# First feed-forward: six plain tile pairs, then sixteen pairs by seven block products

## The chip, the cores and the metric

One core of one Trainium2 chip runs the whole program in one launch. The metric is the device time in microseconds (us), the median of several runs. The engines are PE (matmul), DVE, ACT and POOL (elementwise), and SP, which issues the loads from HBM; PEld is PE's weight load.

## The reference, cut to what matters

The program is three transformer-like blocks over 512 tokens of width 1024. The change touches the feed-forward of the first:

```python
D_FF = 2816
def swiglu(h, w1, w2):
    g, u = jnp.split(h @ w1, 2, axis=-1)
    return (jax.nn.silu(g) * u) @ w2
...
h_lat = h_lat + g2 * swiglu(modulate(rms_norm(h_lat, norm2_g[l]), sh2, sc2),
                            w_ffn_in[l], w_ffn_out[l])
```

Beside it the kernel computes modulation rows for later use, `silu(c) @ w_ada + b_ada` (the sixth group of the first block's and the three groups `w_ada_3` of the third block's), as running sums of 128x1024 rows.

## The kernel before

**Numbers.** Everything is held transposed, features on the 128 partitions and 512 tokens along a row. A float32 operand is held as two parts, high (rounded to fp32r) and low (the rest). A product is three matmuls: high x high, high x low and low x high (L1477 to L1479 for 512 columns). A weight tile of 128x1024 is loaded to one of five buffers (`raw`, t_53; `NRAW` = 5, L206), cast by ACT (L1914) and subtracted by POOL (L3179), which gives its high and low part. The event `read` of a load is the end of its last reader. `send` (L1333) issues load number n only after `read` of load n - 5; SP does this in order. ACT casts the tile two ahead in its own order (`LOOK`).

**The feed-forward.** There are 22 pairs: gate tile g(i) and up tile u(i), 8 input tiles each. `ffn` (L687) takes them in two parts, each followed by the output products (e and d) over the middle tiles of that part. There are two forms:
- `plain` (L757), in the first block's feed-forward (tag ff1) alone, in parts of 14 and 8 pairs: 48 matmuls of 512 columns a pair. Behind the products come silu on ACT (L2218), gate times up on DVE (L2949), the high part on ACT (L2006), the low part on DVE (L2422).
- `fours` (L802), in the four feed-forwards of the second block, in parts of 8 and 14 pairs. Gate, up and the two halves of the tokens form a 2x2 block product that is done by seven block products p1, p5, p6, p7, p4, p2, p3 in this order: 84 matmuls of 256 columns (L1513 to L1515). The seven weight pieces of a pair (A11, S1, S2, S3, A22, A12, S4) are 128x512: S1 to S4 are sums made by DVE from both raw tiles of the pair (U the upper, L the lower), L2432, L2435, L2445; pieces are cast by ACT (L1929) and their low parts made by POOL (L3189) or DVE (L2452). The results are put together on DVE: `second_sum`, `third_sum`, `up_sum` (L2472; p3 waits for it), `last_sum` (L2477), L2484 (a scaling that ff1 doesn't have), `pair_up` (L2494), `mid_low` (L2422). The pieces of pair i+1 are made during pair i. In DVE's queue S1 of pair i+1 stands ahead of `second_sum` and `up_sum` of pair i.

**Order.** It is written out by hand in the loops. Each engine is in order. The generator `modulations` (L545) makes one step each time `next(m.side)` is called: eight steps with one load of w_ada (R) and one sum on DVE (L2543 for the first, L2546), an empty one, and one that closes the group (16 small matmuls on PE, L1782, and one DVE add). The sums' `read` frees their raw buffer. In ff1 it is called once in each pair from the fourth on, and two to four times beside each output tile.

**Weight parts.** Three buffers for high and low parts are taken in turn in ff1, four in the other feed-forwards (`rotate`); a block piece takes half of one.

## Time and profile before

| | us |
|---|---|
| median of three runs | 3389.88 (3387.67 to 3390.45) |
| the profiled execution, its own time | 3392.9 |
| its span | 3391.1 |
| first matmul of ff1 to the first of the next block | 835.46 to 1208.42 |

Starts in the rows are in us from the span's start. A line number is the line that issued an instruction. In square brackets stands the idle time of the engine before a row, and what ended it.

### The profile page before, as it was taken

The numbers are of one execution on the slowest core, as the hardware profiler recorded it, in microseconds if no ns is written. First come the engines' busy times: TensorE is split into PE (matmuls) and PEld (weight loads), VectorE is DVE, ScalarE is ACT, GpSimd is POOL, SyncE is SP. The second block draws the span as 40 slices with busy tenths as digits, with TensorE's granted clock in tenths as the row PEclk, the third lists the DMA queues.
The fourth block names the chain that finished last, engine by engine and source line by source line (L and its number), as shares of the span: only waits on it lengthen the run. The fifth ranks groups of instructions, "written<-read, shape, count | busy, mean of one in ns | idle before, by whom it ended". The sixth has DMA issues, their size and how long they took to land.

```text
span 3391.1 us, 47136 instructions
## 1 busy us (share of the span) xinstructions
PE 3309.1 (98%) x18750; PEld 2794.0 (82%) x18750; DVE 1872.6 (55%) x3335; ACT 1416.2 (42%) x2517; POOL 1680.6 (50%) x996
## 2 busy tenths in 40 slices
PE   8999999999999999999999999999999989999998
PEld 5767788887888898988777999899987769998776
DVE  4266775433222386842667576557624667682655
ACT  4533323423322353533445354444434455352643
POOL 4323445554544455655525565565646346564432
PEclk9999999999999999999999999999999999999999
DMA  7212334442344423234312323332343113233221
GB/s 285 69 51 63 95 98 131 148 143 75 123 154 137 151 94 100 100 104 116 85 35 89 102 100 105 95 112 88 107 109 111 32 60 116 96 109 99 73 63 56
DMA packets 102218, 345.95 MB, mean 102 GB/s; under 512 B 12174, under 2 KB 12558, under 8 KB 101839
## 3 DMA queue, kind: packets, MB, share of 16 engines
q1 hardware_dynamic: 101200, 341.10, 31.4%
q8 instruction: 148, 2.42, 0.3%
q10 hardware_dynamic: 798, 1.85, 0.2%
q14 instruction: 72, 0.58, 0.1%
HBM read 336.08 MB, written 2.10 MB: 100 GB/s over the span
## 4 chain that ended last, share of the span: by engine, by line
PE 88%; DVE 5%; ACT 3%; POOL 1%; DMA 1%; issue 1%; SPq 0%; DVEq 0%; ACTq 0%
PE ps L1477 17%; PE ps L1479 16%; PE ps L1478 16%; PE ps L1513 8%; PE ps L1514 8%; PE ps L1515 8%; PE ps L1540 2%; PE ps L1541 2%; PE ps L1542 2%; PE ps L1827 2%; PE ps L1854 1%; PE ps L1837 1%; ACT t L1929 1%; PE ps L1746 1%; POOL t L3179 1%
## 5 line engine op out<-in xcount | busy, mean ns | idle before, releaser
L3179 POOL TENSOR_TENSOR t<-t,t 128x1024 fp32r<-128x1024 f32 (+2 forms) x408 | 923.2, 2269 | 1162.2 <-ACT t L1914 1153.0
L1477 PE MATMUL ps<-t,t 128*128 128x512 f32 x2608 | 1046.2, 401 | 11.6 <-POOL t L3179 5.9
L1479 PE MATMUL ps<-t,t 128*128 128x512 f32 x2608 | 1026.1, 393 | 0.0
L1478 PE MATMUL ps<-t,t 128*128 128x512 f32 x2608 | 1025.1, 393 | 0.0
L3189 POOL TENSOR_TENSOR t<-t,t 128x512 fp32r<-128x512 f32 x440 | 572.2, 1329 | 361.7 <-ACT t L1929 361.7
L1513 PE MATMUL ps<-t,t 128*128 128x256 f32 x2464 | 695.7, 282 | 18.4 <-POOL t L3189 7.1
L1514 PE MATMUL ps<-t,t 128*128 128x256 f32 x2464 | 694.9, 282 | 0.0
L1515 PE MATMUL ps<-t,t 128*128 128x256 f32 x2464 | 693.7, 282 | 0.0
L1477 PEld LDWEIGHTS ps<-t,t 128*128 128x128 f32 x2608 | 493.1, 189 | 140.7 <-issue 23.9
L1479 PEld LDWEIGHTS ps<-t,t 128*128 128x128 f32 x2608 | 492.3, 189 | 110.3
L1478 PEld LDWEIGHTS ps<-t,t 128*128 128x128 f32 x2608 | 493.1, 189 | 103.8 <-issue 1.7
L1914 ACT CAST t<-t 128x1024 fp32r<-128x1024 f32 (+2 forms) x412 | 398.9, 977 | 359.8 <-PE ps L1479 223.0
L1513 PEld LDWEIGHTS ps<-t,t 128*128 128x128 f32 x2464 | 466.4, 189 | 24.3 <-POOL t L3189 10.2
L1515 PEld LDWEIGHTS ps<-t,t 128*128 128x128 f32 x2464 | 466.6, 189 | 0.0
L1514 PEld LDWEIGHTS ps<-t,t 128*128 128x128 f32 x2464 | 465.1, 189 | 0.3
L1929 ACT CAST t<-t 128x512 fp32r<-128x512 f32 x440 | 255.5, 620 | 201.6 <-DVE t L2445 180.9
L2259 ACT ACTIVATE t<-ps,t 128x128 f32<-128x128 f32 (+3 forms) x160 | 86.6, 545 | 199.4 <-DVE t L3021 86.7
L1929 ACT CAST t<-ps 128x512 fp32r<-128x512 f32 x176 | 103.5, 588 | 145.0 <-DVE ps L2435 106.6
L2722 DVE SCALAR_TENSOR_TENSOR ps<-t,t,ps 128x392 f32<-128x392 f32 (+14 forms) x232 | 159.1, 686 | 6.2
L2445 DVE TENSOR_TENSOR t<-t,ps 128x512 f32<-128x512 f32 x176 | 120.2, 683 | 48.4 <-PE ps L1515 44.0
L1540 PE MATMUL ps<-t,t 128*128 128x512 f32 x336 | 134.9, 401 | 5.4 <-DVE t L2630 2.8
L2452 DVE TENSOR_TENSOR t<-ps,t 128x512 fp32r<-128x512 f32 x176 | 120.9, 687 | 30.8 <-ACT t L1929 27.8
(325 smaller groups left out, 3613.3 us busy)
## 6 DMA issues: line engine op xcount, KB each, us to landing
t<-in_w_f1i SPq DMA_DIRECT2D x88, 512.0 KB, 3.8
t<-in_w_f2i SPq DMA_DIRECT2D x88, 512.0 KB, 3.7
t<-in_w_ada SPq DMA_DIRECT2D x72, 512.0 KB, 4.3
t<-in_w_ffi SPq DMA_DIRECT2D x44, 512.0 KB, 3.7
t<-in_w_f1o SPq DMA_DIRECT2D x32, 512.0 KB, 4.0
t<-in_w_f2o SPq DMA_DIRECT2D x32, 512.0 KB, 4.1
t<-in_w_gate SPq DMA_DIRECT2D x24, 512.0 KB, 4.2
t<-in_w_out SPq DMA_DIRECT2D x48, 256.0 KB, 2.6
```

The lines of the kernel that those rows point to most:

```text
L1477: e.matmul(out, wh[:, at], X.hi[c][:, 0:N], start=c == first, stop=False)
L1478: e.matmul(out, wh[:, at], X.lo[c][:, 0:N], start=False, stop=False)
L1479: m = e.matmul(out, wl[:, at], X.hi[c][:, 0:N], start=False, stop=c == final)
L1513: e.matmul(out, wh[:, at], m.A.hi(j, x), start=opens and j == 0, stop=False, skip_group_check=not opens)
L1514: e.matmul(out, wh[:, at], m.A.lo(j, x), start=False, stop=False, skip_group_check=not opens)
L1515: mm = e.matmul(out, wl[:, at], m.A.hi(j, x), start=False, stop=j == 3, skip_group_check=not opens)
L1540: e.matmul(out, X.hi[c][:, at], wh[:, w], start=c == 0, stop=False)
L1914: e.copy(k.WH[k.slot[n]][:, 0:w], k.raw[:, j % NRAW, 0:w]).then_inc(*k.rounded.inc(('rounded', j)))
L1929: e.copy(four(piece_at(k, k.WH, m, i, piece)), src).then_inc(*k.rounded.inc(('rounded', m.tag, i, piece)))
L2722: e.scalar_tensor_tensor((c3 if j == 30 else a3)[:, :, lo:hi], h3[:, :, lo + w - 15:hi + w - 15], param(k, 'conv_w', w * 8 + i), a3[:, :, ...
L3179: e.tensor_tensor(k.WL[k.slot[n]][:, 0:w], k.raw[:, j % NRAW, 0:w], f(k.WH[k.slot[n]][:, 0:w]), ALU.subtract).then_inc(*k.rest.inc(('rest' ...
L3189: e.tensor_tensor(four(piece_at(k, k.WL, m, i, piece)), src, four(f(piece_at(k, k.WH, m, i, piece))), ALU.subtract).then_inc(*k.rest.inc(( ...
```

## The change

ff1 is now six plain pairs (0 to 5) and then block pairs: 6 and 7 in part 0, 8 to 21 in part 1, so that the output tiles take 8 middle tiles in part 0 and 14 in part 1 (before 14 and 8).

The block form needs sums of input blocks (t1 to t4, `Turned`). They are made beside pairs 1 to 4 by `turn_even` and `turn_odd`: per step four copies on ACT (512, 256, 512 and 256 columns) and ten sums on DVE (four of 512 and six of 256 columns), ordered around `ffn_gate` and `ffn_up`. The first four pieces of pair 6 are begun beside pair 5 (`begin_pair`).

`next(m.side)` is called twice in each of the six plain pairs, twice beside each output tile of part 0, once in each of the pairs 8 to 13, and as before in part 1's output tiles. Silu of a block pair reads PSUM directly. The ring of temporary tiles for the middle is three instead of four.

```diff
@@ -204,7 +229,7 @@
 
 
 NRAW, LOOK, LEAD = (5, 2, 2)
-PARTS, PAIRS = (((0, 14), (14, 8)), ((0, 8), (8, 14)))
+PAIRS, PLAIN = (((0, 8), (8, 14)), 6)
 PIECES = ('A11', 'S1', 'S2', 'S3', 'A22', 'A12', 'S4')
 PRODUCTS = {'p1': ('A11', 'b11', 'A', 0), 'p5': ('S1', 't1', 'D', 256), 'p6': ('S2', 't2', 'B', 0), 'p7': ('S3', 't3', 'C', 0), 'p4': ('A22', 't4', 'D', 0), 'p2': ('A12', 'b21', 'A', 0), 'p3': ('S4', 'b22', 'D', 256)}
 SUMS = ('b11', 't1', 't2', 't3', 't4', 'b21', 'b22')
@@ -318,6 +343,13 @@
     k.MH, k.ML = k.MH + k.MH[0:8], k.ML + k.ML[0:8]
     high = sbuf(k, [128, 4, 7 * 256], F32R, at=k.halves)
     first, outer, low = sbuf(k, [128, 1024], F32R, at=k.halves + 28 * 1024), place(k, 0, [128, 768], F32R), place(k, 3, [128, 3, 7 * 256], F32R)
+    turned, last = place(k, -6, [128, 30, 256], F32R), place(k, 88, [128, 2, 256], F32R)
+    sets = []
+    for j in range(7):
+        p = 4 * j
+        sets.append([turned[:, p, :], turned[:, p + 1, :], turned[:, p + 2, :], turned[:, p + 3, :], turned[:, p + 1:p + 3, :].rearrange('p a n -> p (a n)')])
+    sets.append([last[:, 0, :], turned[:, 28, :], turned[:, 29, :], last[:, 1, :], turned[:, 28:30, :].rearrange('p a n -> p (a n)')])
+    k.TH, k.TL = (sets[0:4], sets[4:8])
     k.SUMH = [high[:, j, :] for j in range(4)]
     k.SUML = [(first, outer)] + [(low[:, j, 0:1024], low[:, j, 1024:1792]) for j in range(3)]
 
@@ -633,16 +665,16 @@
     m = Norm(res.sum, k.X, lambda j: ('x', 'out1', j), A, lambda j: k.sm[:, j:j + 1], lambda j: k.ada[:, 24 + j:25 + j], [('filled', ('out1', 7)), ('gain2',)], keep=True, bank=True)
     for j in range(11):
         norm(on, m, j)
-    twin = short(banked(Sum('f1_0', k.R[0], S, ('normed', 'n2', 7), range(8), 0, [('lo', ('mid', 'ff1'), FF - 1)])))
-    first = banked(Sum('fin1', k.R[1], S, ('normed', 'cn', 7), range(8)))
+    twin = short(banked(Sum('f1_0', k.R[0], S, ('filled', ('u', 'ff1', FF - 1)), range(8), 0, [('lo', ('mid', 'ff1'), FF - 1)])))
+    first = banked(Sum('fin1', k.R[1], S, ('filled', ('u', 'ff1', FF - 1)), range(8)))
     first.slots = twin.slots
     on.final_gain()
     on.twin_gain('final_g', 2)
     res = Residual('ff1', lambda j: k.ada[:, 40 + j:41 + j], first, [('ada', 'ada', 5)], None, Sums(k, 'f1_0'), lambda j: k.sm[:, 16 + j:17 + j], twin, lambda j: k.sm[:, 24 + j:25 + j])
-    m = Ffn('ff1', 'ffi', 'ffo', A, None, res, [('filled', ('out1', 7))], side=side)
+    m = Ffn('ff1', 'ffi', 'ffo', A, None, res, [('filled', ('out1', 7))], side=side, clear=('filled', ('out1', 7)))
+    m.sums, m.start = (Turned(k, A), PLAIN)
     m.next = Ffn('f1_0', 'f1i0', 'f1o0', res.A, twin, None, [('filled', ('d', 'ff1', 7))], res, clear=('filled', ('out1', 7)), before=res)
     ffn(on, k, m)
-    on.rotate(8, 0)
     return m.next
@@ -660,13 +692,14 @@
     def __init__(self, tag, wi, wo, A, scale, res, since, whole=None, side=iter(()), clear=None, before=None):
         self.tag, self.wi, self.wo, self.A, self.scale, self.res, self.since, self.whole = (tag, wi, wo, A, scale, res, since, whole)
         self.side, self.next, self.clear, self.before = (side, None, clear, before)
+        self.sums, self.start = (A, 0)
 
     def again(self, i):
 
         return [('filled', ('e', self.tag, KT - 1))] if i >= 14 else []
 
...
@@ -686,9 +719,12 @@
 
 def ffn(on, k, m):
     m.mid = Pair(('mid', m.tag), k.MH, k.ML)
-    for part, (first, count) in enumerate(PARTS if m.scale is None else PAIRS):
-        (plain if m.scale is None else fours)(on, m, first, count)
-        after = (m.next, 0) if part else (None if m.scale is None else m, first + count)
+    for part, (first, count) in enumerate(PAIRS):
+        if first < m.start:
+            plain(on, m)
+            on.rotate(8, 0)
+        fours(on, m, max(first, m.start), first + count - max(first, m.start))
+        after = (m.next, 0) if part else (m, first + count)
         for n in range(KT):
             on.T(('ed'[part], m.tag, n), m.wo, n, m.mid, kt=count, first=first)
             for _ in range(n < 4 if part else 2):
@@ -754,17 +790,25 @@
         on.add_squares(res, n)
 
 
-def plain(on, m, first, count):
-    for i in range(first, first + count):
+def plain(on, m):
+    for i in range(m.start):
         if i:
             on.T(('g', m.tag, i), m.wi, i, m.A)
         else:
             on.T2((('g', m.tag, 0), m.wi, 0), (('u', m.tag, 0), m.wi, FF), m.A)
         on.ffn_gate(m, i)
+        if 0 < i < 5:
+            on.turn_even(m, i - 1)
+        if i == m.start - 1:
+            begin_pair(on, m, m.start, KT - 2)
         if i:
             on.T(('u', m.tag, i), m.wi, FF + i, m.A)
         on.ffn_up(m, i)
-        if i > 2:
+        if 0 < i < 5:
+            on.turn_odd(m, i - 1)
+        if i == m.start - 1:
+            begin_pair(on, m, m.start, KT - 1)
+        for _ in range(2):
             next(m.side, None)
 
 
@@ -860,6 +904,8 @@
             on.round(m, i + 1, 'S4')
             on.minus(m, i + 1, 'S4')
         on.product(m, i, 'p3')
+        if 7 < i < 14:
+            next(m.side, None)
         if m.whole is not None and i == 2:
             on.roots(m.whole.sum, 1)
         if m.whole is not None and i == 3:
...
@@ -1509,10 +1559,10 @@
             self.wait_ge('up sum', m.tag, i)
         for j in js:
             at = slice(128 * j, 128 * j + 128)
-            self.wait_ge('lo', m.A.tag, j, x)
-            e.matmul(out, wh[:, at], m.A.hi(j, x), start=opens and j == 0, stop=False, skip_group_check=not opens)
-            e.matmul(out, wh[:, at], m.A.lo(j, x), start=False, stop=False, skip_group_check=not opens)
-            mm = e.matmul(out, wl[:, at], m.A.hi(j, x), start=False, stop=j == 3, skip_group_check=not opens)
+            self.wait_ge(*m.sums.ready(j, x))
+            e.matmul(out, wh[:, at], m.sums.hi(j, x), start=opens and j == 0, stop=False, skip_group_check=not opens)
+            e.matmul(out, wh[:, at], m.sums.lo(j, x), start=False, stop=False, skip_group_check=not opens)
+            mm = e.matmul(out, wl[:, at], m.sums.hi(j, x), start=False, stop=j == 3, skip_group_check=not opens)
         if js[-1] == 3:
             mm.then_inc(*k.filled.inc(('used', m.tag, i, piece), ('filled', (p, m.tag, i)), *([('filled', ('u', m.tag, i))] if p == 'p3' else [])))
 
@@ -1916,7 +1974,7 @@
     def round(self, m, i, piece):
 
         k, e = (self.k, self.e)
-        if i == 0:
+        if i == m.start:
             self.wait_ge(*m.clear)
         for event in k.before.get((m.tag, i, piece), ()):
             self.wait_ge(*event)
@@ -1931,14 +1989,22 @@
     def first_copy(self, m, i):
         k, e = (self.k, self.e)
         self.wait_ge('filled', ('p1', m.tag, i))
-        if i:
+        if i > m.start:
             self.wait_ge('last sum', m.tag, i - 1)
+        elif m.start:
+            self.wait_ge('normed', m.A.tag, 7)
         else:
             self.wait_ge('x', m.before.tag, 7)
         e.copy(k.tmp[3][:, 0:256], self.bank('A', m.tag, i)[:, 0:256]).then_inc(*k.act.inc(('first copy', m.tag, i)))
 
     def pair_gate(self, m, i):
-        self.ffn_gate(m, i)
+        k, e = (self.k, self.e)
+        if m.scale is not None:
+            self.ffn_gate(m, i)
+            return
+        b = self.take(m.ring(k), 'm', m.tag, i)
+        self.wait_ge('last sum', m.tag, i)
+        e.activation(b, self.bank('A', m.tag, i), ACT.Silu).then_inc(*k.act.inc(('silu', m.tag, i), ('free', ('A', m.tag, i))))
 
     def pair_up(self, m, i):
         self.high(m.mid, i, self.bank('C', m.tag, i), ('up', m.tag, i), *m.since, *m.again(i))
@@ -2177,6 +2243,22 @@
         else:
             e.activation(A.hi(j, 'b21', 2), x, ACT.Copy, scale=g).then_inc(*k.act.inc(('hi', A.tag, j, 'b2')))
 
+    def turn_even(self, m, j):
+        k, e, A, T, b = (self.k, self.e, m.A, m.sums, self.bank('G', m.tag, j))
+        self.lent('G', m.tag, j)
+        self.wait_ge('lo', A.tag, 2 * j + 1)
+        e.copy(pairs(b), f(k.HH)[:, 2 * j:2 * j + 2, 256:512]).then_inc(*k.act.inc(('turn high', j)))
+        for event in (m.clear, ('filled', ('row', A.tag))):
+            self.wait_ge(*event)
+        self.wait_ge('turned', j, 't1')
+        e.copy(T.hi(j, 't1'), b[:, 0:256]).then_inc(*k.act.inc(('hi', A.tag, j, 't1')))
+
+    def turn_odd(self, m, j):
+        k, e, A, T, b, c = (self.k, self.e, m.A, m.sums, self.bank('G', m.tag, j), self.bank('H', m.tag, j))
+        self.wait_ge('turned', j, 't4')
+        e.copy(T.hi(j, 't2', 2), b).then_inc(*k.act.inc(('hi', A.tag, j, 't2')))
+        e.copy(T.hi(j, 't4'), c[:, 0:256]).then_inc(*k.act.inc(('hi', A.tag, j, 't4')))
+
     def sum_highs(self, res, n):
 
         k, e, A, j, b = (self.k, self.e, res.A, n // 2, self.bank('G', res.A.tag, n // 2))
@@ -2478,6 +2560,8 @@
 
     def pair_gate(self, m, i):
         k, e = (self.k, self.e)
+        if m.scale is None:
+            return
         b = self.take(m.ring(k), 'm', m.tag, i)
         self.wait_ge('row', m.scale.tag)
         self.wait_ge('last sum', m.tag, i)
@@ -2835,6 +2919,36 @@
         if j % 2:
             self.low(A, j, self.k.O[:, j, :])
 
+    def turn_even(self, m, j):
+
+        k, e, A, T, b = (self.k, self.e, m.A, m.sums, self.bank('G', m.tag, j))
+        self.wait_ge('turn high', j)
+        e.tensor_tensor(b, b, f(A.hi[2 * j]), ALU.subtract).then_inc(*k.dve.inc())
+        self.settle()
+        e.tensor_tensor(pairs(b), pairs(b), f(k.HL)[:, 2 * j:2 * j + 2, 256:512], ALU.add).then_inc(*k.dve.inc())
+        self.settle()
+        e.tensor_tensor(b, b, f(A.lo[2 * j]), ALU.subtract).then_inc(*k.dve.inc(('turned', j, 't1')))
+
+    def turn_odd(self, m, j):
+
+        k, e, A, T, b, c = (self.k, self.e, m.A, m.sums, self.bank('G', m.tag, j), self.bank('H', m.tag, j))
+        one, three, hi, lo = (b[:, 0:256], c[:, 0:256], f(A.hi[2 * j + 1]), f(A.lo[2 * j + 1]))
+        self.wait_ge('hi', A.tag, j, 't1')
+        e.tensor_tensor(T.lo(j, 't1'), one, f(T.hi(j, 't1')), ALU.subtract).then_inc(*k.dve.inc(('lo', A.tag, j, 't1')))
+        self.settle()
+        e.tensor_tensor(one, hi[:, 256:512], one, ALU.subtract).then_inc(*k.dve.inc())
+        self.settle()
+        e.tensor_tensor(one, lo[:, 256:512], one, ALU.add).then_inc(*k.dve.inc())
+        self.settle()
+        self.lent('H', m.tag, j)
+        e.tensor_tensor(three, hi[:, 0:256], one, ALU.subtract).then_inc(*k.dve.inc())
+        self.settle()
+        e.tensor_tensor(three, lo[:, 0:256], three, ALU.add).then_inc(*k.dve.inc(('turned', j, 't4')))
+        self.wait_ge('hi', A.tag, j, 't2')
+        e.tensor_tensor(T.lo(j, 't2', 2), b, f(T.hi(j, 't2', 2)), ALU.subtract).then_inc(*k.dve.inc(('lo', A.tag, j, 't2'), ('lo', A.tag, j, 't3'), ('free', ('G', m.tag, j))))
+        self.wait_ge('hi', A.tag, j, 't4')
+        e.tensor_tensor(T.lo(j, 't4'), three, f(T.hi(j, 't4')), ALU.subtract).then_inc(*k.dve.inc(('lo', A.tag, j, 't4'), ('free', ('H', m.tag, j))))
+
     def sum_parts(self, res, n):
 
         k, e, A, g, j, x, b = (self.k, self.e, res.A, res.g(n), n // 2, self.k.X[:, n, :], self.bank('G', res.A.tag, n // 2))
```

SP's queue at the start of ff1. Tile t_53 is the five raw buffers, in_w_ffi the gate and up weights, in_w_ada the modulation rows. Before:

```order
L1341 DMA t_53<-in_w_out 128x1024 x8
L1341 DMA t_53<-in_w_ffi 128x1024 x8
L1341 DMA t_53<-in_w_ada 128x1024
L1341 DMA t_53<-in_w_ffi 128x1024 x2
L1341 DMA t_53<-in_w_ada 128x1024
L1341 DMA t_53<-in_w_ffi 128x1024 x2
```

With the change:

```order
L1391 DMA t_53<-in_w_out 128x1024 x8
L1391 DMA t_53<-in_w_ffi 128x1024 x2
L1391 DMA t_53<-in_w_ada 128x1024 x2
L1391 DMA t_53<-in_w_ffi 128x1024 x2
L1391 DMA t_53<-in_w_ada 128x1024 x2
L1391 DMA t_53<-in_w_ffi 128x1024 x2
L1391 DMA t_53<-in_w_ada 128x1024 x2
L1391 DMA t_53<-in_w_ffi 128x1024 x4
```

Two ada loads now follow each pair's two weight loads; before, eight weight loads came first and one ada load per pair after them.

DVE's queue from the product of pair 1 to that of pair 2 (t_63 and t_64 are middle tiles, t_126 the turned sums, t_50 and t_51 the input's high and low parts, t_56 the running sum). Before:

```order
L2949 TENSOR_TENSOR t_63<-t_63,ps 128x512 [waits s_act,s_filled]
L2422 TENSOR_TENSOR t_121<-t_63,t_120 128x512 [waits s_act]
L2949 TENSOR_TENSOR t_64<-t_64,ps 128x512 [waits s_act,s_filled]
L2422 TENSOR_TENSOR t_121<-t_64,t_120 128x512 [waits s_act]
```

With the change:

```order
L3063 TENSOR_TENSOR t_63<-t_63,ps 128x512 [waits s_filled]
L2504 TENSOR_TENSOR t_121<-t_63,t_120 128x512 [waits s_act]
L2937 TENSOR_TENSOR t_126<-ps,t_126 128x256
L2939 TENSOR_TENSOR ps<-t_50,ps 128x256 [waits s_dve]
L2941 TENSOR_TENSOR ps<-t_51,ps 128x256 [waits s_dve]
L2944 TENSOR_TENSOR ps<-t_50,ps 128x256 [waits s_dve]
L2946 TENSOR_TENSOR ps<-t_51,ps 128x256 [waits s_dve]
L2948 TENSOR_TENSOR t_126<-ps,t_126 128x512 [waits s_act]
L2950 TENSOR_TENSOR t_126<-ps,t_126 128x256 [waits s_act]
L2630 SCALAR_TENSOR_TENSOR t_56<-t_53,t_60,t_56 128x1024 [waits s_raw4]
L2630 SCALAR_TENSOR_TENSOR t_56<-t_53,t_60,t_56 128x1024 [waits s_dve,s_raw0]
L2926 TENSOR_TENSOR ps<-ps,t_50 128x512 [waits s_act]
```

The two sums of ada loads (s_raw4, s_raw0) stand behind the pair's product, its low part and the turned sums.

DVE's queue around the end of the block pair 8, with the change (t_65 holds the partial results, t_64 a middle tile):

```order
L2554 TENSOR_TENSOR ps<-ps,t_65 128x512 [waits s_dve,s_filled]
L2527 TENSOR_TENSOR t_55<-t_53,ps 128x512 [waits s_dve,s_filled]
L2627 TENSOR_SCALAR t_56<-t_53,t_60 128x1024 [waits s_raw1]
L2559 TENSOR_TENSOR ps<-ps,t_65 128x256 [waits s_filled]
L2514 TENSOR_TENSOR ps<-t_53 128x512 [waits s_raw1,s_raw0,s_act]
L2578 TENSOR_TENSOR ps<-t_64,ps 128x512 [waits s_dve]
```

These are up_sum, S4 of the next pair, the ada sum, last_sum, S1 of the pair after, pair_up. The ada sum and S1 use the same raw buffer (s_raw1). Before, ff1 had no block pairs, and no block pair elsewhere has an ada sum.

## Rows read from the trace of the kernel before

**Rows 1.** The page: span, busy time of PE, the chain's share by engine.
```profile
span 3391.1 us, 47136 instructions
...
PE 3309.1 (98%) x18750; PEld 2794.0 (82%) x18750; DVE 1872.6 (55%) x3335; ACT 1416.2 (42%) x2517; POOL 1680.6 (50%) x996
...
PE 88%; DVE 5%; ACT 3%; POOL 1%; DMA 1%; issue 1%; SPq 0%; DVEq 0%; ACTq 0%
```

**Rows 2.** Timeline of DVE, plain pairs: start, duration, line, tiles, idle before.
```profile
852.24 0.69 DVE L2422 TENSOR_TENSOR t<-t,t 128x512 fp32r<-128x512 f32 x1 [0.69 <-ACT t L2006]
860.03 0.69 DVE L2949 TENSOR_TENSOR t<-t,ps 128x512 f32<-128x512 f32 x1 [7.10 <-PE ps L1479]
861.41 0.69 DVE L2422 TENSOR_TENSOR t<-t,t 128x512 fp32r<-128x512 f32 x1 [0.69 <-ACT t L2006]
870.91 0.69 DVE L2949 TENSOR_TENSOR t<-t,ps 128x512 f32<-128x512 f32 x1 [8.81 <-PE ps L1479]
...
881.79 0.69 DVE L2949 TENSOR_TENSOR t<-t,ps 128x512 f32<-128x512 f32 x1 [8.81 <-PE ps L1479]
...
883.77 1.28 DVE L2546 SCALAR_TENSOR_TENSOR t<-t,t,t 128x1024 f32<-128x1024 f32 x1
```

**Rows 3.** Timeline of DVE, block pairs of the second block.
```profile
1399.80 0.43 DVE L2477 TENSOR_TENSOR ps<-ps,t 128x256 f32<-128x256 f32 x1 [0.73 <-PE ps L1515]
...
1400.88 1.81 DVE L2432 TENSOR_TENSOR ps<-t 128x512 f32<-128x512 f32 x1
...
1407.13 0.69 DVE L2472 TENSOR_TENSOR ps<-ps,t 128x512 f32<-128x512 f32 x1
1408.31 0.69 DVE L2445 TENSOR_TENSOR t<-t,ps 128x512 f32<-128x512 f32 x1 [0.49 <-PE ps L1515]
1409.73 0.43 DVE L2477 TENSOR_TENSOR ps<-ps,t 128x256 f32<-128x256 f32 x1 [0.72 <-PE ps L1515]
...
1419.65 0.43 DVE L2477 TENSOR_TENSOR ps<-ps,t 128x256 f32<-128x256 f32 x1 [0.75 <-PE ps L1515]
```

**Rows 4.** SP's timeline, and time to landing of ffi's 44 loads.
```profile
885.08 0.33 SPq L1341 DMA_DIRECT2D t<-in_w_ffi  x1
...
DMA to landing us min/median/max: 3.4/3.7/5.8
```

**Rows 5.** Timeline of ACT in plain pairs, and one copy in a block pair.
```profile
852.12 1.05 ACT L1914 CAST t<-t 128x1024 fp32r<-128x1024 f32 x1
854.59 0.60 ACT L2218 ACTIVATE t<-ps 128x512 f32<-128x512 f32 x1 [1.43 <-PE ps L1479]
...
1401.53 0.36 ACT L1938 COPY t<-ps 128x256 f32<-128x256 f32 x1
```

**Rows 6.** Timeline of POOL, splits of weight tiles in plain pairs.
```profile
853.24 2.39 POOL L3179 TENSOR_TENSOR t<-t,t 128x1024 fp32r<-128x1024 f32 x1 [1.90 <-ACT t L1914]
...
884.16 3.15 POOL L3179 TENSOR_TENSOR t<-t,t 128x1024 fp32r<-128x1024 f32 x1 [3.81 <-ACT t L1914]
```

**Rows 7.** Timeline of PE, one of the four closings of a modulation group.
```profile
957.76 1.84 PE L1782 MATMUL ps<-t 128*128 128x2 f32 x16
```

**Rows 8.** Timeline of DVE beside an output tile of ff1, two ada sums.
```profile
1044.65 4.62 DVE L2546 SCALAR_TENSOR_TENSOR t<-t,t,t 128x1024 f32<-128x1024 f32 x2
```

**Rows 9.** Groups of DVE by line, 1345 to 1475 us: busy, mean ns, idle.
```profile
L2432 DVE TENSOR_TENSOR ps<-t 128x512 f32<-128x512 f32 x12 | 17.1, 1425 | 0.0
L2435 DVE TENSOR_TENSOR ps<-ps,t 128x512 f32<-128x512 f32 x13 | 9.1, 700 | 0.4
```

**Rows 10.** PE's timeline at ff1's start; busy by engine, granted clock, DMA there.
```profile
835.46 0.77 PE L1477 MATMUL ps<-t,t 128*128 128x512 f32 x1 [2.45 <-DVE t L2592]
...
829.00:840.00 11.00, 6.62 (x21) 5.44 (x21) 7.05 (x12) 4.99 (x8) 0.00 (x0) 0.53 0.01 2
```

**Rows 11.** The same view by stretches, the next blocks' first pairs.
```profile
1208.00:1224.00 16.00, 13.37 (x105) 12.48 (x104) 14.30 (x25) 9.50 (x19) 9.77 (x7) 1.00 0.19 66
2172.00:2188.00 16.00, 13.36 (x105) 12.48 (x104) 13.98 (x22) 7.42 (x15) 8.55 (x6) 1.00 0.23 67
```

30 lines of the change are left out of this document (27 added, 3 removed).

## The prediction

> **What bounds the kernel now.** I read the page's head first [rows 1]: TensorE (PE) is busy 98% of the span and holds 88% of the chain that ended last; DVE, ACT and POOL are near half. A change pays only through the length of PE's queue or through PE's waits. So I went to the first block's feed-forward, 835 to 1208 us, and asked two things: how long a pair (one gate and one up tile) takes PE in either form, and how near the other engines are to making PE wait.
>
> Pace. In the plain tiles the gate-times-up product on DVE (L2949) stands at 860.03, 870.91, 881.79 [rows 2]: 10.88 us a pair, 48 products of 512 columns, with PE busy for all of it. In block form the last sum (L2477) stands at 1399.80, 1409.73, 1419.65 [rows 3]: 9.93 us for 84 products of 256 columns. I use those distances and not counts of matmul records, since some records are missing. A pair saves 0.95 us, not an eighth of 10.88 (1.36), because a short product pays its fixed part more often.
>
> Waits. Weights pass through five load buffers. A load may be issued only when the load five before it has been read. The trace shows this wait: DVE reads an ada load from 883.77 for 1.28 us [rows 2], and SP issues the next ffi load at 885.08 [rows 4], 0.03 us later. A load lands 3.7 us after issue (median) [rows 4]; then ACT's cast (1.05) and POOL's subtraction (2.4) must end before PE may use it: 3.51 us from 852.12 to 855.63 [rows 5, 6]. So a load is usable 7.2 us after its buffer is read. Before, with one ada load per pair, and only from pair 3, the load five later has over a pair of room and PE never waits for it.
>
> **The change, part by part.**
>
> Sixteen pairs in block form: 16 x 0.95 = 15.2 us off PE's queue (14 to 16 by the spread of the distances). The output tiles keep 176 x 3 products. Four closings of 1.84 us on PE [rows 7] stay four.
>
> Two ada loads in each of pairs 0, 1, 2, 4 and 5. The loads now run g, u, R, R (R an ada load; L and U for a block pair are below), four a pair, so g of pair i+2 takes the buffer of the second R of pair i. That R is read by DVE behind all DVE work of pair i, which begins when pair i is complete on PE. Its g must be usable one pair (10.88) later. Room for DVE: 10.88 - 7.2 = 3.7 us. What stands there: the product, the wait for ACT's high part and the low part, 2.1 us (860.03 to 862.10) [rows 2], and two ada sums of 1.28: 4.6 already. With turn_odd: six sums of 256 columns at about 0.43, one of 512 at 0.69, a 0.6 us ACT copy between [rows 2, 3, 5]: 4 us more.
> - Pair 2: R0b follows the low part that ends at 852.93, so it is read at 855.5, g2 usable at 862.8; pair 1 ends at 860.0 (its product on DVE is at 860.03). Wait 2.9 us (2.5 to 3.5).
> - Pair 3: ACT stands in order at the cast of g2 till 859.2, before silu of pair 1 and the first turn copy. Then follow cast 1.05, silu 0.6, copy 0.6, turn_even's three sums (2.1), copy 0.4, the cast of u2, product and high and low, turn_odd 4, two ada sums: R1b is read near 872.5, g3 usable at 879.8, against 862.8 + 10.88 = 873.7. Wait 6.1 us (4.5 to 8).
> - Pair 3 issues no R (its steps are an empty one and a closing), so g4 takes u2's buffer and u4 R2a's: both are usable 0.5 to 2 us early, and pair 5 likewise.
> - Pair 6, the first block pair: U6 takes R4b's buffer. DVE after pair 4: 2.1 + 4 + 2.6, so U6 lands 12.4 us after pair 4's end; A11 needs ACT 0.6 and POOL 1.3 more: 14.4 against 10.88, wait 3.5. S2 comes behind pair 5's product on DVE: 1.5. L7 takes R5a's buffer, read after that: S1 of pair 7 stands in DVE's queue until L7 lands, and up_sum of pair 6, for which p3 waits, is behind it: 4.6. Together 9.6 (3.2 to 12). The low end has no late load: A11's first half buffer is last used by u5, so cast and subtraction (2.0) are exposed anyway, with 1.2 for S2.
>
> Output tiles of part 0: now 5.44 us each with three loads, before 9.7 with four. Two ada sums took 4.62 us there against 2 x 1.28 alone [rows 2, 8]. With the 0.75 us residual step that is 5.4 of 5.44 us. I take 1.5 us (0 to 6).
>
> Pairs 8 to 13: one R each, between L of i and U of i+1. L of i+2 takes R of i's buffer. DVE's order in a pair: last_sum(i-1), S1(i+1), product(i-1), and so on to up_sum(i), S4(i+1), the ada sum. Measured from a pair's start on PE (1399.7): up_sum ends at 8.1 and p3 may begin at 8.5; S4 runs 8.6 to 9.3 [rows 3]. So the ada sum ends at 10.6 or later, 0.6 into the next pair; L lands at 4.4; S1 starts then instead of at 1.2; from its end to up_sum's end was 5.13 us (1402.69 to 1407.82) back to back [rows 3]: 10.2 + 0.1 against 8.5: p3 waits 1.8 us, and the next pair repeats it. S1, with both inputs in SBUF, takes 1.42 us on the mean against 0.68 to 0.70 for sums from PSUM [rows 9]; an ada sum has the same inputs, so I take 2.0 a pair (0 to 2.4). Only L10 to L14 are hit (o7 is in front of L9's slot, L13 in front of L15's): 5 x 2.0 = 10.0.
>
> The Trainium skill, "SBUF — State Buffer", section "SBUF: two separate sides", says that a DVE operation with two SBUF inputs and a GpSimd operation exclude each other for a whole instruction. The trace agrees: POOL's split under an ada sum took 3.15 against 2.40 [rows 6]. By that rule alone every ada sum could wait out a split of 2.4, which would put the case at the dear rival's time below.
>
> Clock. Where PE last waited in pieces, 2.45 us before 835.46 among them, the granted clock was 0.53 over 829 to 840, the 1.2 GHz level for nearly all of it [rows 10]: up to 5 us for one such stretch. The new gaps are as long or longer. Where a late load sets the next start anyway the slower PE is hidden; after pair 3's start it isn't. I take 3 us (0 to 10). The skill's "TensorE: Matmul & The Clock Gate", section "HAM oscillation — how this bites in real kernels", has the same rule against waiting PE; by it the first three waits would each bring a slow stretch, 5 us more than my sum.
>
> The next block's first pair: 1208 to 1224 and 2172 to 2188 have the same PE busy time (13.37, 13.36) [rows 11], the first behind eight-part, the second behind fourteen-part output tiles. So the longer tiles of part 1 buy nothing there: 0 (-1 to +1). The rings of three instead of four, the priors of the two square sums and the rotation are free: what they wait for is long done.
>
> Sum: 2.9 + 6.1 + 9.6 + 1.5 + 10.0 + 3.0 = 33.1 of waits, less 15.2: **+17.9 us**. The profiled execution took 3392.9 us with a span of 3391.1; the median of the three runs is 3389.9, and against it this gives **3407.8**.
>
> **The rivals.**
> - *No buffer is late* (faster). It needs DVE to read the second ada load within 3.7 us of a pair's end. Then only pair 6's 3.2 us stay: 3389.9 - 15.2 + 3.2 = 3378. For it: DVE had stood idle 8.81 us before the product at 870.91 [rows 2]. Against it: that idle time lies before PE ends the pair, and the work behind that point is 8.7 us long. 0.11.
> - *The inner waits are absorbed.* The plain tiles and pair 6 behave as forecast, but S1's delay in pairs 9 to 13 hides in DVE's idle 1.4 us a pair and less work without a scaled gate: 10 less, 3398, down to 3393 if pair 6 is cheap too. 0.17.
> - *Collisions and clock come dear*: each ada pair 4.6 us (+2 at pairs 2, 3, 6), output tiles +4, clock +5: 3423. 0.16.
> - *Nothing moves* (the extra waits come to just the saving): 3390. It needs waits of half my sum. 0.06.
>
> **How the numbers follow.** Forecast 0.50: 3400 to 3416 by its own bounds. The likeliest is 3407.8. Leaving out the fast rival and part of the dear one, 3391 to 3424 holds 8 in 10. A measurement can tell some 0.2% (6.8 us) from no change. Faster: 0.11. Within: 0.06 and a third of the absorbed case, 0.12. Slower: the rest, 0.77.
>
> **What the profile after would show.** L2949's successors no longer 10.88 apart: gaps before pairs 2 and 3 of 3 and 6 us, with ACT waiting for a DMA of ffi and POOL for ACT. In the block pairs 9 to 13, 11.9 us between last sums, PE's p3 waiting for up_sum, S1 idle before it for a DMA; pairs 14 to 21 at 9.93. PE's queue is 576 matmuls longer. If pairs 2 and 3 start on time, the reading of the five buffers is wrong and the fast rival holds.

## The result, and the profile after

The changed kernel takes **3433.98 us** (median of four runs, 3430.47 to 3435.73) against 3390.16 of the kernel before, run beside it: a ratio of 1.0122, 95% interval 1.011 to 1.0135. The forecast was 3407.8 with a range of 3391 to 3424: the sign was right, the size was not, and the time lies 10 us above the range. The profiled executions differ by 39.4 us (spans of 3430.5 and 3391.1).

The page of the changed kernel, the rows that answer to [rows 1]:

```profile
span 3430.5 us, 48764 instructions
...
PE 3308.1 (96%) x19326; PEld 2817.3 (82%) x19326; DVE 2000.0 (58%) x3535; ACT 1457.7 (42%) x2629; POOL 1703.0 (50%) x1044
...
PE 84%; DVE 8%; ACT 4%; DMA 2%; issue 1%; POOL 1%; SPq 0%; DVEq 0%; ACTq 0%
```

PE is as busy as before (3308 against 3309 us) with 576 matmuls more, and holds 84% of the chain instead of 88%. DVE, ACT and DMA have taken its place: PE waits more. Where, the stretches show (us, busy time of each engine with its count, granted clock, DMA share). They are the plain pairs, pairs 6 and 7, the output tiles of part 0, pairs 8 to 21, the output tiles of part 1:

```profile
833.86:928.58 94.72, 74.82 (x304) 59.86 (x305) 55.00 (x75) 28.44 (x45) 27.72 (x13) 0.90 0.30 100
928.58:958.82 30.24, 24.37 (x168) 23.58 (x169) 17.61 (x25) 11.77 (x20) 18.35 (x11) 0.88 0.38 122
958.82:1008.76 49.94, 48.71 (x226) 39.39 (x225) 26.21 (x26) 9.29 (x11) 16.03 (x7) 1.00 0.59 200
1008.76:1162.55 153.79, 143.12 (x1178) 142.07 (x1178) 113.20 (x170) 75.51 (x137) 98.07 (x71) 0.99 0.37 119
1162.55:1242.83 80.28, 79.74 (x354) 65.01 (x353) 31.99 (x58) 33.60 (x55) 32.75 (x16) 1.00 0.34 101
```

ff1 takes 408.97 us from its first product to the next block's, before 372.96: 36.0 of the 39.4 us. Before, the same six plain pairs took 68.0 us (835.46 to 903.47); now 94.7, one closing among it.

PE's timeline, the rows with a wait before pairs 2 and 3, before and in pair 6, and in pair 10:

```profile
862.45 0.80 PE L1527 MATMUL ps<-t,t 128*128 128x512 f32 x1 [4.06 <-POOL t L3293]
...
883.19 0.77 PE L1527 MATMUL ps<-t,t 128*128 128x512 f32 x1 [7.16 <-POOL t L3293]
...
928.58 0.56 PE L1563 MATMUL ps<-t,t 128*128 128x256 f32 x1 [7.79 <-POOL t L3303]
934.28 0.39 PE L1563 MATMUL ps<-t,t 128*128 128x256 f32 x1 [0.89 <-DVE t L2534]
936.61 0.39 PE L1563 MATMUL ps<-t,t 128*128 128x256 f32 x1 [0.63 <-POOL t L3303]
938.83 0.39 PE L1563 MATMUL ps<-t,t 128*128 128x256 f32 x1 [0.55 <-POOL t L3303]
945.74 0.36 PE L1563 MATMUL ps<-t,t 128*128 128x256 f32 x1 [3.79 <-DVE ps L2554]
...
1042.90 0.35 PE L1563 MATMUL ps<-t,t 128*128 128x256 f32 x1 [2.84 <-DVE ps L2554]
```

The places are those of the forecast. The waits before pairs 2, 3 and 6 are longer than forecast (4.06, 7.16 and 7.79 us against 2.9, 6.1 and 3.5); the four inside pair 6 come to 5.9 against 6.1. What stands behind the one before pair 3, on DVE, SP, ACT and POOL (L3063 is gate times up, [rows 2]; L2504 the low part; L2630 two ada sums):

```profile
863.07 0.68 DVE L3063 TENSOR_TENSOR t<-t,ps 128x512 f32<-128x512 f32 x1
865.06 2.44 DVE L2504 TENSOR_TENSOR t<-t,t 128x512 fp32r<-128x512 f32 x1 [1.32 <-ACT t L2072]
871.29 2.66 DVE L2630 SCALAR_TENSOR_TENSOR t<-t,t,t 128x1024 f32<-128x1024 f32 x2
...
873.98 19.59 SPq L1391 DMA_DIRECT2D t<-in_w_ffi  x4
...
879.58 1.04 ACT L1972 CAST t<-t 128x1024 fp32r<-128x1024 f32 x1 [8.99 <-DMA t<-in_w_ffi]
...
864.59 2.37 POOL L3293 TENSOR_TENSOR t<-t,t 128x1024 fp32r<-128x1024 f32 x1 [2.19 <-ACT t L1972]
880.70 2.35 POOL L3293 TENSOR_TENSOR t<-t,t 128x1024 fp32r<-128x1024 f32 x1 [13.74 <-ACT t L1972]
```

DVE's second ada sum ends at 873.95, SP issues g3 at 873.98, ACT can cast it only 5.6 us later, and POOL's split ends at 883.05: the chain of the forecast, link by link. Two links were longer. The low part took 2.44 us and not 0.69: POOL's split ends at 866.96, and DVE's low part ends 0.54 later. And the load came after 5.6 us, not 3.7 [rows 4]; of the twelve ffi loads from 835 to 960 the median to landing is 6.0.

One sentence of the section on the kernel has to be put right: a step of the modulations is not made "two to four times beside each output tile" but twice beside each tile of part 0 and once beside each of the first four of part 1. The forecast's sum doesn't use it.

### The profile page after: what moved, and what is told of

It reads as the page before. It is cut to its first block, busy times and chain, and to the rows that moved or that the text cites. A ratio compares the mean times of both kernels' runs of the same rounds, so it can differ in the third digit from the quotient of the medians.

```text
span 3430.5 us, 48764 instructions
## 1 busy us (share of the span) xinstructions
PE 3308.1 (96%) x19326; PEld 2817.3 (82%) x19326; DVE 2000.0 (58%) x3535; ACT 1457.7 (42%) x2629; POOL 1703.0 (50%) x1044
## 4 chain that ended last, share of the span: by engine, by line
PE 84%; DVE 8%; ACT 4%; DMA 2%; issue 1%; POOL 1%; SPq 0%; DVEq 0%; ACTq 0%
PE ps L1527 14%; PE ps L1529 14%; PE ps L1528 14%; PE ps L1563 9%; PE ps L1564 9%; PE ps L1565 9%; PE ps L1590 2%; PE ps L1592 2%; PE ps L1591 2%; PE ps L1885 2%; PE ps L1912 1%; DMA t<-in_w_ffi 1%; ACT t L1987 1%; PE ps L1895 1%; DVE t L2630 1%
## 5 line engine op out<-in xcount | busy, mean ns | idle before, releaser
L3293 POOL TENSOR_TENSOR t<-t,t 128x1024 fp32r<-128x1024 f32 (+1 forms) x376 | 837.4, 2235 | 1088.4 <-ACT t L1972 1078.9
L1527 PE MATMUL ps<-t,t 128*128 128x512 f32 x2352 | 949.4, 404 | 24.8 <-POOL t L3293 18.9
L1529 PE MATMUL ps<-t,t 128*128 128x512 f32 x2352 | 927.8, 394 | 0.0
L1528 PE MATMUL ps<-t,t 128*128 128x512 f32 x2352 | 927.2, 394 | 0.0
L3303 POOL TENSOR_TENSOR t<-t,t 128x512 fp32r<-128x512 f32 x520 | 680.3, 1336 | 452.1 <-ACT t L1987 452.1
L1563 PE MATMUL ps<-t,t 128*128 128x256 f32 x2912 | 825.8, 284 | 44.0 <-DVE ps L2554 20.1
L1564 PE MATMUL ps<-t,t 128*128 128x256 f32 x2912 | 823.9, 283 | 0.0
L1565 PE MATMUL ps<-t,t 128*128 128x256 f32 x2912 | 822.7, 283 | 0.0
L1563 PEld LDWEIGHTS ps<-t,t 128*128 128x128 f32 x2912 | 554.6, 190 | 52.4 <-issue 30.3
L1527 PEld LDWEIGHTS ps<-t,t 128*128 128x128 f32 x2352 | 446.2, 190 | 146.4 <-issue 33.9
L1565 PEld LDWEIGHTS ps<-t,t 128*128 128x128 f32 x2912 | 554.3, 190 | 0.0
L1564 PEld LDWEIGHTS ps<-t,t 128*128 128x128 f32 x2912 | 552.9, 190 | 0.3
L1529 PEld LDWEIGHTS ps<-t,t 128*128 128x128 f32 x2352 | 445.4, 189 | 100.3
L1528 PEld LDWEIGHTS ps<-t,t 128*128 128x128 f32 x2352 | 446.4, 190 | 93.5 <-issue 1.7
L1972 ACT CAST t<-t 128x1024 fp32r<-128x1024 f32 (+2 forms) x380 | 364.7, 971 | 334.3 <-PE ps L1529 180.5
L1987 ACT CAST t<-t 128x512 fp32r<-128x512 f32 x520 | 302.4, 620 | 249.5 <-DVE t L2527 217.4
L2527 DVE TENSOR_TENSOR t<-t,ps 128x512 f32<-128x512 f32 x208 | 141.8, 682 | 54.3 <-PE ps L1565 49.3
L2534 DVE TENSOR_TENSOR t<-ps,t 128x512 fp32r<-128x512 f32 x208 | 142.7, 686 | 35.6 <-ACT t L1987 31.8
L2514 DVE TENSOR_TENSOR ps<-t 128x512 f32<-128x512 f32 x104 | 139.5, 1341 | 27.4 <-DMA t<-in_w_ffi 27.2
```

Source lines behind the costliest of these rows:

```text
L1527: e.matmul(out, wh[:, at], X.hi[c][:, 0:N], start=c == first, stop=False)
L1528: e.matmul(out, wh[:, at], X.lo[c][:, 0:N], start=False, stop=False)
L1529: m = e.matmul(out, wl[:, at], X.hi[c][:, 0:N], start=False, stop=c == final)
L1563: e.matmul(out, wh[:, at], m.sums.hi(j, x), start=opens and j == 0, stop=False, skip_group_check=not opens)
L1564: e.matmul(out, wh[:, at], m.sums.lo(j, x), start=False, stop=False, skip_group_check=not opens)
L1565: mm = e.matmul(out, wl[:, at], m.sums.hi(j, x), start=False, stop=j == 3, skip_group_check=not opens)
```

## The experiments

Theory 1 is the forecast's: late modulation reads keep load buffers from weight tiles. Theory 2: the turned sums and the block form's own work make PE wait, whatever the loads. Theory 3: DVE or DMA can't carry that many loads a pair, in any order. All ratios below are against the kernel before, which took 3392.86 to 3393.00 us beside these runs, with the 95% interval.

Behind ff1 all these kernels have the same code. Yet from ff1's end to the end of the program the profiled executions took 2182.7 us in the kernel before, 2187.7 in the changed one, and 2182.7 to 2188.2 in the runs below. So some us of each median come from outside ff1, and an edit is better read by ff1's own length (408.97 us in the changed kernel), which stands with each run.

**Both kernels without most modulation loads.** The edit, the same in both:

```diff
                 for kt in range(KT):
-                    on.ada_sum(name, g, kt)
+                    (kt in (0, 7) or (name, g) in (('ada', 2), ('ada', 3), ('ada', 4))) and on.ada_sum(name, g, kt)
                     yield
...
-            self.wait_ge('ada part', name, g, kt - 1)
+            self.wait_ge('ada part', name, g, kt - 1 if (name, g) in (('ada', 2), ('ada', 3), ('ada', 4)) else 0)
```

> The changed kernel with work left out: of the modulation group that is summed in ff1 and of the three groups of the third block only the first and the last row (kt 0 and 7) are loaded and summed, so 24 loads and 24 DVE sums are gone and the order of all else stays. Theory 1 (late loads: a modulation load that DVE reads late holds the buffer of a weight load): nothing is late in pairs 2, 3 and 9 to 13, block form is worth its 15.2 us less 3 to 5 at pair 6, and this kernel takes 3375 to 3382 us, some 55 less than with all loads (3434). Theory 2 (the turned sums and the block form's own DVE and POOL work make PE wait, whatever the loads): pairs 2 and 3 still wait 3 us or more each and the time stays above 3400.

> The kernel before with the same 24 loads and sums left out. Both theories: its pairs are 10.88 us apart with or without them, so 3387 to 3390 us, the base against which the other cut kernel is read. The distance between the two cut kernels is what block form itself brings: 10 to 12 us by theory 1, none or less than none by theory 2.

The changed kernel so cut took 3385.83 us (0.9979, 0.997 to 0.9989), the one before 3391.51 (0.9993, 0.9984 to 1.0003), both above what was expected (3375 to 3382, and 3387 to 3390). The stretches of the changed one:

```profile
835.20:907.21 72.01, 69.46 (x304) 57.05 (x305) 42.73 (x71) 29.26 (x46) 27.94 (x13) 0.97 0.26 88
907.21:929.75 22.54, 21.79 (x169) 21.62 (x169) 12.77 (x21) 11.08 (x19) 16.48 (x11) 0.92 0.38 121
929.75:977.63 47.88, 47.88 (x227) 39.64 (x225) 15.08 (x17) 9.06 (x11) 16.58 (x7) 1.00 0.31 109
977.63:1118.51 140.88, 140.49 (x1178) 140.32 (x1178) 107.27 (x165) 76.04 (x137) 93.50 (x71) 1.00 0.34 112
```

The loads, their sums and what they trigger are the loss: 48 us by the medians (3434.0 to 3385.8), 45.4 of them in ff1 (408.97 to 363.59). The waits before pairs 2 and 3 are gone, the turned sums still made. That speaks against theory 2. But block form itself brings only 5.7 us between the two cut kernels, not the 10 to 12 expected. In ff1 it is 8.5 (372.10 against 363.59), which adds up: 16 x 0.87 = 13.9, since the last sums of L2559 stand 10.01 apart here and not 9.93 [rows 3]; less 2.1 for the wait for the first block piece (907.21, the low end of the forecast for pair 6), 2.5 in pairs 6 and 7, 0.8 in pairs 8 to 21. The other 2.8 us are lost outside ff1, as shown below.

The cut changed kernel also shows DVE and POOL meeting, with no load in the way (low parts L2504; splits L3293):

```profile
861.15 0.85 DVE L2504 TENSOR_TENSOR t<-t,t 128x512 fp32r<-128x512 f32 x1 [0.69 <-ACT t L2072]
872.03 1.56 DVE L2504 TENSOR_TENSOR t<-t,t 128x512 fp32r<-128x512 f32 x1 [0.69 <-ACT t L2072]
882.92 2.25 DVE L2504 TENSOR_TENSOR t<-t,t 128x512 fp32r<-128x512 f32 x1 [0.69 <-ACT t L2072]
...
859.05 2.40 POOL L3293 TENSOR_TENSOR t<-t,t 128x1024 fp32r<-128x1024 f32 x1 [3.65 <-ACT t L1972]
870.64 2.40 POOL L3293 TENSOR_TENSOR t<-t,t 128x1024 fp32r<-128x1024 f32 x1 [2.13 <-ACT t L1972]
882.24 2.38 POOL L3293 TENSOR_TENSOR t<-t,t 128x1024 fp32r<-128x1024 f32 x1 [1.33 <-ACT t L1972]
```

The splits end at 861.45, 873.04 and 884.62, the low parts at 862.00, 873.59 and 885.17: always 0.55 us later, whenever the low part began. It doesn't run slower; it stands still until POOL is done. The rule of the Trainium skill that the forecast weighed ("SBUF — State Buffer", "SBUF: two separate sides") says this: a DVE operation with two SBUF inputs and a GpSimd one lock each other out for a whole instruction. The trace agrees.

Such a meeting is also behind the 2.8 us outside ff1. In the next block an operation of DVE (L3158) has two SBUF inputs and takes 0.75 us in the other cut kernel. Here a split begins 0.04 us after it:

```profile
1637.96 2.93 DVE L3158 SCALAR_TENSOR_TENSOR t<-t,t,t 128x512 f32<-128x512 f32 x1
1638.00 2.34 POOL L3293 TENSOR_TENSOR t<-t,t 128x1024 fp32r<-128x1024 f32 x1 [0.43 <-ACT t L1972]
1641.63 0.88 PE L1895 MATMUL ps<-t,t 128*128 128x128 f32 x3 [3.17 <-DVE t L3100]
```

It ends at 1640.89, again 0.55 us after the split. PE waits 3.17 us for the DVE operation behind it, in the other kernel 0.98, and the granted clock of the next 8 us is 0.81, there 1.00: by the end of these products the lead has fallen from 7.7 us to 4.0 in the profiled executions. Whether the two met in every execution isn't recorded.

**Loads one place earlier.**

```diff
             on.T2((('g', m.tag, 0), m.wi, 0), (('u', m.tag, 0), m.wi, FF), m.A)
+        for _ in range(2):
+            next(m.side, None)
         on.ffn_gate(m, i)
...
             begin_pair(on, m, m.start, KT - 1)
-        for _ in range(2):
-            next(m.side, None)
```

> All work is done. In the six plain pairs the two modulation steps stand between the gate and the up tile, no longer behind the up tile; as many loads, one place earlier, and the DVE sums behind the turned sums as before. Theory 1: the buffer that was kept from a gate tile is now kept from an up tile, which is needed 5.44 us later, so a lateness of 4 and 7 us at pairs 2 and 3 becomes 0 to 2, and at pair 6 only 3 to 4 us of the 10 stay: 15 to 24 us less than the changed kernel, 3410 to 3419. Theory 3 (DVE or the DMA queue can't do two loads a pair in any order): less than 5 us of change.

3408.95 us (1.0047, 1.0032 to 1.0062), 25 less than the changed kernel with the same loads and the same work, and 1 below the expected range; ff1 took 389.66 us, 19.3 less. Theory 3 is out for the plain pairs. The stretches of plain pairs and of pairs 6 and 7:

```profile
833.60:915.72 82.12, 72.28 (x304) 58.02 (x305) 61.98 (x79) 29.07 (x46) 30.70 (x13) 0.95 0.36 119
915.72:938.26 22.54, 21.86 (x169) 21.69 (x170) 12.77 (x21) 11.08 (x19) 16.55 (x11) 0.92 0.45 153
```

12.6 us come back in the plain pairs and 7.7 in pairs 6 and 7, which are as short as with the loads left out.

**No loads in pairs 8 to 13.**

```diff
-            for _ in range(n < 4 if part else 2):
+            for _ in range((2, 2, 2, 2, 1, 1, 0, 0)[n] if part else 2):
...
-        if 7 < i < 14:
+        if False:
             next(m.side, None)
```

> The changed kernel with no modulation step in pairs 8 to 13; instead ten steps instead of four beside the output tiles of part 1 (2, 2, 2, 2, 1, 1, 0, 0). All work is done. Pairs 9 to 13 took 12.4 to 13.1 us between last sums where pairs 14 to 21 took 10.0. If the one modulation load a pair is the cause, they come to 10.0: 5 x 2.8 = 14 us less, less one or two half-clock stretches on the way, 2 to 4 us more in the tiles of part 1: 3420 (3416 to 3424). If it is the block form itself (S1 from two SBUF inputs, the read of the turned sums), they stay above 12 and the time at 3431 to 3436.

3420.29 us (1.0082, 1.0068 to 1.0095), 13.7 less, as theory 1 said. Pairs 8 to 21 take 140.88 us instead of 153.79, to 0.01 us what they take with the loads left out; the output tiles of part 1 take 2.6 more, the plain pairs, which the edit leaves as they are, 1.4. ff1 took 400.07 us, 8.9 less.

**The same loads, read one place earlier in DVE's queue in pairs 8 to 13.**

```diff
         on.up_sum(m, i)
+        if 7 < i < 14:
+            next(m.side, None)
         on.product(m, i, 'p2')
...
         on.product(m, i, 'p3')
-        if 7 < i < 14:
-            next(m.side, None)
```

> The changed kernel with the modulation step of pairs 8 to 13 one place earlier in DVE's queue: behind up_sum, ahead of S4 of the next pair, so that DVE reads the load 1.2 us earlier, ahead of S4's wait for p4; the same loads in the same order. If p3 waits because the load behind it in the ring is issued late (SP waits for that read), each of the five pairs gets 1 to 1.3 us shorter (12.8 to 11.6), 5 to 7 us in all, 3427 to 3429. If DVE is simply full in these pairs (its sums take 2.35 us there and not 1.28), nothing changes, within 2 us of 3434.

3425.87 us (1.0099, 1.0086 to 1.0113), 8 less and 1 below the expected range. But ff1 took 406.11 us, only 2.9 less, pairs 8 to 21 in it 3.3 less (150.46 against 153.79): most of the 8 us lies outside ff1, and that the median came near the range is luck. Last sums of L2559 stood 12.78, 13.09, 12.77, 12.41 and 12.88 apart (63.9 us); now 12.06, 13.50, 10.32, 11.91 and 12.18 (60.0). Up to the last sum of pair 14 the gain is 3.3 us. So 3 to 4 us came back here, less than the 5 to 7 expected; a slow stretch lies in these pairs in both kernels (granted clock 0.57 from 1055 to 1059 before the edit, 0.63 from 1043 to 1047 with it). The changed kernel first, then this one:

```profile
1030.16 2.35 DVE L2630 SCALAR_TENSOR_TENSOR t<-t,t,t 128x1024 f32<-128x1024 f32 x1
1032.43 0.42 DVE L2559 TENSOR_TENSOR ps<-ps,t 128x256 f32<-128x256 f32 x1
1036.92 0.70 DVE L2514 TENSOR_TENSOR ps<-t 128x512 f32<-128x512 f32 x1 [4.07 <-DMA t<-in_w_ffi]
...
1042.06 0.69 DVE L2554 TENSOR_TENSOR ps<-ps,t 128x512 f32<-128x512 f32 x1
1042.66 0.68 DVE L2527 TENSOR_TENSOR t<-t,ps 128x512 f32<-128x512 f32 x1
1043.26 2.35 DVE L2630 SCALAR_TENSOR_TENSOR t<-t,t,t 128x1024 f32<-128x1024 f32 x1
```

```profile
1029.74 1.70 DVE L2630 SCALAR_TENSOR_TENSOR t<-t,t,t 128x1024 f32<-128x1024 f32 x1
1031.36 0.67 DVE L2527 TENSOR_TENSOR t<-t,ps 128x512 f32<-128x512 f32 x1
```

The first fence is a closed loop: ada sum 2.35, load 4.4 to S1, 6.4 from S1 to the end of S4, next ada sum. That is 13.1 us from one ada sum to the next, and PE has no part in it but to wait for up_sum. With the ada sum at 1.28 the loop would be 12.0, which is the forecast's 11.9. Moving the read ahead of S4 shortens the loop by S4's 0.6 and by what the sum no longer waits for POOL (1.70, mean 1.65 in these pairs, against 2.35).

**Turned sums shortened.** In `turn_even` and `turn_odd` on DVE:

```diff
-        e.tensor_tensor(pairs(b), pairs(b), f(k.HL)[:, 2 * j:2 * j + 2, 256:512], ALU.add).then_inc(*k.dve.inc())
-        self.settle()
...
-        e.tensor_tensor(one, hi[:, 256:512], one, ALU.subtract).then_inc(*k.dve.inc())
-        self.settle()
-        e.tensor_tensor(one, lo[:, 256:512], one, ALU.add).then_inc(*k.dve.inc())
-        self.settle()
...
-        e.tensor_tensor(three, hi[:, 0:256], one, ALU.subtract).then_inc(*k.dve.inc())
-        self.settle()
-        e.tensor_tensor(three, lo[:, 0:256], three, ALU.add).then_inc(*k.dve.inc(('turned', j, 't4')))
+        e.tensor_tensor(three, hi[:, 0:256], one, ALU.subtract).then_inc(*k.dve.inc(('turned', j, 't4')))
```

> The changed kernel with part of the computation left out: of the seven DVE sums a step between product and product that make the turned blocks the ones that bring in the low part and the second block are gone (one of three in turn_even, three of five in turn_odd), some 2 us of DVE work in each of pairs 1 to 4; copies, final parts and waits stay. If DVE's work behind the pair's end sets when the modulation loads are read and when ACT may go on to its next cast, the gaps before pairs 2, 3 and 6 (4.1, 7.2, 7.8 us) lose some 1.3 us (the sums in turn_odd) each, the inner ones too: 4 to 8 us less, 3426 to 3430. If the gaps are due to slow landings alone, nothing: 3432 to 3436.

3427.12 us (1.01, 1.0086 to 1.0113), 7 less, as expected. PE's waits before pairs 2, 3 and 6:

```profile
863.27 0.80 PE L1527 MATMUL ps<-t,t 128*128 128x512 f32 x1 [3.90 <-POOL t L3285]
...
880.63 0.77 PE L1527 MATMUL ps<-t,t 128*128 128x512 f32 x1 [3.30 <-POOL t L3285]
...
921.31 0.55 PE L1563 MATMUL ps<-t,t 128*128 128x256 f32 x1 [3.21 <-POOL t L3295]
```

Before pair 2, where no turned sum stands ahead of the ada sums, nothing changes (4.06 to 3.90). Before pairs 3 and 6 the wait falls by 3.9 and 4.6 us, three times the 1.3 of DVE work left out behind a pair's end, and more. The traces show where most of the rest comes from. Before pair 3 one sum of `turn_even` (0.7 us) is gone ahead of the product as well, and the load is cast 4.4 us after its issue, not 5.6. Before pair 6 the low part of pair 4 no longer meets a split (0.69 us, not 2.47), and the load is cast 5.3 us after its issue, not 6.0. ff1 took 402.54 us, 6.4 less. DVE work behind a pair's end is on the path, as theory 1 needs.

**Both single edits together.**

> Both single edits together: in the plain pairs the two modulation steps stand between gate and up tile, in pairs 8 to 13 there is none, and ten stand beside the output tiles of part 1. All work is done. The first alone took 25 us off the changed kernel (3434 to 3409), the second 14 (3434 to 3420). If they hit different places, they add: 3395 (3391 to 3399). If both only moved the same DVE or DMA backlog, less than 30 of the 39 us come off: above 3403.

3401.19 us (1.0024, 1.0015 to 1.0034). Of 39 us 33 come off, 6 less than the sum and 2 above the range. In ff1 itself the two edits do add: it takes 377.4 us, 31.6 less than in the changed kernel, where the single edits gave 19.3 and 8.9, together 28.2. The 6 us are missing outside ff1 (the rest behind it took 2186.5 us here, 2184.2 and 2183.7 with the single edits, 2187.7 in the changed kernel).

**One load in each plain pair, none in pairs 8 to 13.** The step stands ahead of the turned sums (shown), or behind them:

```diff
         on.ffn_up(m, i)
+        for _ in range(1):
+            next(m.side, None)
         if 0 < i < 5:
             on.turn_odd(m, i - 1)
...
-        for _ in range(2):
-            next(m.side, None)
...
-            for _ in range(n < 4 if part else 2):
+            for _ in range((3, 3, 3, 3, 2, 2, 0, 0)[n] if part else 2):
...
-        if 7 < i < 14:
+        if False:
             next(m.side, None)
```

> All work is done. One modulation step in each plain pair, ahead of the last turned sums; none in pairs 8 to 13; the twelve steps that are left out there stand beside the output tiles of part 1 (3, 3, 3, 3, 2, 2, 0, 0 steps for tiles 0 to 7). Theory 1: no weight load is late in any pair, only pair 6 waits 3 to 5 us: 3376 to 3383, faster than both kernels. Against it: the 9.5 us output tiles with three steps could become too short for DVE (3 x 2.3 us where each sum meets a POOL split, and the residual's own work, 3 to 4): then up to 10 us more, 3390.

> As the kernel with one modulation step in each plain pair and none in the block pairs (3399 us), but the step stands behind the last turned sums, no longer ahead of them: DVE reads the load some 3.5 us later, the turned copies and with them ACT's next cast come 1.3 us earlier. By the ring of five buffers the load is now kept from the up tile two pairs on: read 9 to 10 us after the pair's end, usable 7.2 to 9 us later, 16.3 to 19 against 16.3: 0 to 2 us of wait in each of pairs 3 to 5. By ACT's queue (its cast of the next gate tile stands behind the turned copies) the waits of 1.1 and 1.6 us in pairs 4 and 5 go. So 3394 to 3404; the places of the gaps tell the two apart: at an up tile, with ACT waiting for a DMA, or at a gate tile, with POOL waiting for ACT.

3398.94 us (1.0015, 1.0005 to 1.0024) ahead, 3400.55 (1.0025, 1.0015 to 1.0035) behind. The first missed its forecast (3376 to 3383) by 16 us; the two can't be told apart. In the first ff1 takes 376.7 us, 13.1 more than with the loads left out: 3.3 in the plain pairs, 1.2 in pairs 6 and 7, 1.0 and 4.5 in the output tiles of part 0 and 1, 3.2 in pairs 8 to 21 (a closing of 1.84 us, which stands in the plain pairs there and in part 1 here, taken out of both). So the output tiles of part 1, to which the loads had been moved, took the largest share; the expectation had warned of that, but with 3390 at most. The second was to tell the ring from ACT's queue and did not: both kinds of wait are in it (ACT waits 3.6 us for three ffi loads, PE 2.9 us in three waits for POOL's split of a gate tile). The second lies in its expected range (3394 to 3404); its ff1 took 380.3 us, pairs 6 and 7 in it 28.2 and in the first 23.7.

**Better places.** Steps per plain pair ahead of the gate's silu and behind the product, and per output tile of part 1; none in the block pairs:

| | ahead | behind | part 1 |
|---|---|---|---|
| first | 3, 2, 0, 0, 0, 0 | 0, 0, 0, 0, 0, 1 | 3, 2, 3, 2, 2, 2, 2, 0 |
| second | 2, 2, 0, 0, 0, 0 | 0, 0, 0, 0, 1, 1 | 3, 3, 2, 2, 2, 2, 2, 0 |

```diff
+        for _ in range((2, 2, 0, 0, 0, 0)[i]):
+            next(m.side, None)
         on.ffn_gate(m, i)
...
         on.ffn_up(m, i)
+        for _ in range((0, 0, 0, 0, 1, 1)[i]):
+            next(m.side, None)
```

> All work is done. Modulation steps where DVE stood idle: three in pair 0 and two in pair 1, ahead of the product, one in pair 5 ahead of its end; none in pairs 2 to 4, none in pairs 6 to 21; two beside each output tile of part 0, and 3, 2, 3, 2, 2, 2, 2, 0 beside those of part 1. The kernel with the loads left out needed 363.6 us from ff1's first product to the next block's, the one before 373.0, the one with a step in each plain pair 376.7. With no DVE sum beside turned sums the plain pairs should take 72 as with the loads left out, pair 6 and 7 23, the rest 1 to 5 us more than there: 366 to 370, that is 3383 to 3389 on the median. It is wrong if the output tiles of part 1 cost more than 3 us: then no better than the kernel before.

> All work is done. Two modulation steps ahead of the product in pairs 0 and 1, one in pairs 4 and 5, none in 2, 3 and the block pairs, 16 beside the output tiles of part 0 and 16 beside those of part 1, there with each closing as the last step of its tile (3, 3, 2, 2, 2, 2, 2, 0). The version with three in pair 0 lost 2.6 us at pair 1, where the third load stood ahead of g1 in SP's queue, and 2.1 at an output tile where two sums followed a closing; both should go: ff1 in 371 to 373 us and 3388 to 3394 on the median, equal to the kernel before. If the output tiles of part 1 still take 86 us and not 80, it stays at 3397 or more.

The first took 3401.29 us (1.0024, 1.0014 to 1.0033; ff1 376.8), 12 above its range. The sign of being wrong that its expectation named came true: leaving out the closing that stands there in addition, the output tiles of part 1 took 4.2 us more than with the loads left out (86.4 against 80.3). The second took 3395.56 (1.0004, 0.9996 to 1.0013): no difference from the kernel before that can be measured, 1.6 above its range, with ff1 in 372.5 us as expected. The gap at the output tile of part 1 went; the one at pair 1 stayed, so my reason for it (SP's queue) was wrong. POOL, DVE and PE there, in the second:

```profile
844.42 1.24 POOL L3337 TENSOR_SCALAR t<-t,t 128x8 f32<-128x8 f32 x1 [19.24 <-DVE t L2656]
845.74 2.67 POOL L3324 TENSOR_TENSOR t<-t,t 128x8 f32<-128x8 f32 x1
848.37 4.70 POOL L3295 TENSOR_TENSOR t<-t,t 128x1024 fp32r<-128x1024 f32 x2
...
844.23 2.67 DVE L2632 SCALAR_TENSOR_TENSOR t<-t,t,t 128x1024 f32<-128x1024 f32 x2
...
850.87 0.47 PE L1529 MATMUL ps<-t,t 128*128 128x512 f32 x1 [2.19 <-POOL t L3295]
```

In the changed kernel the two small operations of POOL took 0.28 and 1.65 us, and the split began 10.8 us after ff1's first product. Here DVE's ada sums, in DVE's idle time, stand against them: 1.24 and 2.67, and the split begins 12.8 us after the first product, 2.0 later. DVE was idle there, and its sums still cost PE time, by way of POOL: it waits 2.19 us here, 0.81 in the changed kernel and 0.41 with the loads left out. In the output tiles of part 1 the ada sums take 2.32 us on the mean (eleven).

No version with all the work beats the kernel before.

## Why the prediction was right in sign and wrong in size

The terms, forecast and measured in ff1 (us):

| term | forecast | measured | from |
|---|---|---|---|
| 16 block pairs | -15.2 | -13.9 | last sums 10.01 apart in pairs 14 to 21 |
| before pair 2 | 2.9 | 4.1 | PE's wait |
| before pair 3 | 6.1 | 7.2 | PE's wait |
| pair 6 | 9.6 | 13.7 | 7.79, 0.89, 0.63, 0.55, 3.79 |
| pairs 9 to 13 | 10.0 | 12.9 | last sums to pair 14, less 6 x 10.01 |
| clock | 3.0 | 10.3 | rest of plain pairs (5.9) and of pairs 6, 7 (4.4) |
| output tiles | 1.5 | 1.7 | rest |
| sum | 17.9 | 36.0 | |
| outside ff1 | 0 | 3.4 | spans: 5.0 more behind ff1, 1.6 less ahead of it |

The rows of the clock and of the output tiles are remainders, so the measured column adds up by construction. Pair 2, pair 6 and pairs 9 to 13 lie above their own bounds (3.5, 12 and 12 us), all to one side: the collision and the late landing below are in each of them.

- **The mechanism** stands: the ring of five buffers, the places of the waits, DVE's order behind the pair's end, S1 held by the load. The runs with the loads left out, one place earlier, out of pairs 8 to 13, and read earlier each moved the stretch that the ring says they would, though not always by the amount expected.
- **The step that failed most is the clock, a term of the sum taken far too small**: "Where a late load sets the next start anyway the slower PE is hidden; after pair 3's start it isn't. I take 3 us". The stretches behind the four longest waits (length, PE's busy time first, the granted clock third from the end):

```profile
861.00:867.00 6.00, 4.55 (x11) 3.59 (x12) 4.62 (x5) 1.83 (x3) 3.77 (x2) 0.50 0.00 1
882.00:888.00 6.00, 4.81 (x11) 3.80 (x12) 4.61 (x5) 1.84 (x3) 3.42 (x2) 0.50 0.00 0
926.00:932.00 6.00, 3.42 (x16) 3.45 (x17) 3.20 (x4) 2.10 (x4) 1.26 (x1) 0.50 0.17 70
946.20:949.40 3.20, 3.20 (x17) 3.20 (x16) 0.43 (x1) 1.16 (x2) 3.20 (x3) 0.50 0.02 5
```

  These 21 us at the lower of the two levels, 1.2 GHz, can cost half their length, 10.6, and the rest that the waits leave is 10.3. PE's busy time for the same products shows 7.9 of it (74.82 and 24.37 us here, 69.46 and 21.79 with the loads left out); the other 2.4 can hold things besides the clock. So the clock cost 8 to 10 us and not 3, and little of it was hidden. The reason, argued and not tried alone: DVE's chain to the ada sums starts when PE ends the pair, so a slow PE makes the next late load later too. The rule of the Trainium skill in "TensorE: Matmul & The Clock Gate", section "HAM oscillation — how this bites in real kernels", that PE's waits bring slow stretches, was the better guide; with the 5 us more that the prediction put on it the term would have been 8.
- **"the product, the wait for ACT's high part and the low part, 2.1 us"** was read from pairs in which POOL's split had not begun [rows 2, 6]. Here it stands at the cast of the same moment: 0.68, 1.32 and 2.44 to 2.47, 4.4 to 4.5 us in each of pairs 1 to 4.
- **"an ada sum has the same inputs, so I take 2.0 a pair (0 to 2.4)"**: the sum took 2.35 us and not 1.28, the loop 12.8 and not 11.9, the loss 2.6 a pair. The row was there [rows 8]: 4.62 for two.
- **"So a load is usable 7.2 us after its buffer is read"** took the median landing of the kernel before, 3.7 [rows 4], where loads mostly came singly. Here an ada load goes out 1.4 us ahead of each late one and more loads right behind it, and it was 5.4 to 6.0 us from issue to cast: g2 853.57 and 858.93, g3 873.98 and 879.58, U6 920.51 and 926.48. With the low part this is why the wait before pair 6 was 7.8 and not 3.5.
- **The saving** of 0.95 us a pair [rows 3] was 0.87 in ff1: 1.3 us.
- **The rivals.** What came is the third, "Collisions and clock come dear", but its number doesn't follow from its terms: 13 us more for five ada pairs, 2 to 6 for pairs 2, 3 and 6, 4 for the output tiles and 5 for the clock, on top of 3407.8, come to 3432 to 3436 and not 3423. That 3434 lies there is luck: the five ada pairs cost 2.9 us more than forecast and the output tiles 0.2; the clock and the late landings made up for them. "The inner waits are absorbed" is refuted by pairs 9 to 13, "No buffer is late" by pairs 2 and 3. Taking each collision at its row should have been in the forecast and not only in a rival.
- **Outside ff1** 3.4 us were lost, with the same code. Behind ff1 it is 5.0, and 3.4 of them go in one place: from 1689 to 1720 PE waited 2.8 us in three waits for DVE, before 1.3 in one, as DVE had waited 3.36 us for a DMA copy and not 1.63; from 1710 to 1718 the granted clock was 0.79, before 1.00 at the same products (1675.8 to 1683.8). Some 620 us behind ff1, past that place, the kernels of the experiments lie up to 4 us apart (at 621.6 to 625.5 us from ff1's end), so this can't be put down to the change.
- **Open**: why that copy came late. Also open is how the 16 us by which the version with one load a pair missed divide between collisions and the clock.

## What to carry to other kernels

When loads of two kinds share a ring, a load that is read late costs the load that many places behind it. Write down, for each late reader, which load takes its buffer and when that one is needed. The duration of a DVE operation with two SBUF inputs holds only for the POOL work it was measured beside: for an operation moved beside POOL's splits, take the row where it met one. A wait of PE of several us is to be counted with the slow stretch behind it, above all where the wait's own loop begins at PE's end. And when an edit touches one stretch of a long program, compare that stretch in the traces beside the medians: here up to 5 us of a median came from elsewhere.

## What the runs showed of the hardware

- A DVE operation with both inputs in SBUF ends 0.55 us after the POOL operation that it meets, whenever it began (0.85, 1.56, 2.25 and 2.44 us for 128x512, which takes 0.69 alone; 2.93 us for the one outside ff1, which takes 0.75 alone). It goes the other way too: POOL operations of 128x8 took 1.24 and 2.67 us instead of 0.28 and 1.65 beside two ada sums.
- The ffi loads of 512 KB from 835 to 960 us landed after 6.0 us (median of twelve, close behind one another and behind ada loads), and after 4.0 with most ada loads left out.
- Block pairs were 10.01 us apart in ff1 in every kernel where nothing was late, and 9.93 in the second block [rows 3]. No run tells why.
